# Modulation sums of an MLP stage: halves of the accumulated blocks move past a stationary block of ones, and the rows come back through memory

## The chip, the cores and the metric

One of the eight NeuronCores of a Trainium2 chip runs the whole program in one launch. The metric is the time of one execution on the device in microseconds (us). Engines are named as in the profile: PE is TensorE (matmul), PEld its loads of stationary tiles, DVE VectorE, ACT ScalarE, POOL GpSimd, SP SyncE, which here only issues DMAs. Each engine takes its instructions in the order of its own list and waits on semaphores.

## The reference, cut to what matters

Two transformer blocks of two layers each run on 512 tokens of width 1024; the second also carries 256 context tokens. The first block ends each of its layers with an MLP, and the second block modulates its activations by twelve vectors a layer that come from two condition vectors:

```python
# first block, each layer, 512 tokens: w1 1024x4096, w2 4096x1024
a = relu(h @ w1); x = x + (a * a) @ w2
# second block, each of two layers; c: latent condition, c_ctx: context condition
mod = silu(c) @ ada_w[layer] + ada_b[layer]      # 1024 -> 6144, for both conditions
sh1, sc1, g1, sh2, sc2, g2 = split(mod, 6)
hx = rmsnorm(x, norm1_g) * (1 + sc1) + sh1       # and so on
```

The matrix ada_w is 1024x6144 a layer, 24 MB. The modulation of layer l of the second block depends on no activation, so it can be computed at any time before that layer.

## The kernel before, in words

Activations lie as 128 features on the partitions, 8 groups, 512 tokens in a row. A product in float32 precision is made of three matmuls of type fp32r: each operand is kept as a rounded high half and a low half (the difference), and high x high, high x low, low x high are summed (TERMS). Weights come in blocks of 1 MB, 128 partitions x 2048, numbered in the order of their use (block s is used in step s of what follows). SP loads a block into STG (two buffers), ScalarE rounds it into the high half of HL (two buffers) in two operations of 1024 columns, VectorE subtracts for the low half, in two operations. The function convert(upto) does this in the ScalarE and VectorE programs; start(u) calls convert(u.i + 1). ScalarE may round block s+2 only when PE has finished with block s, since the buffer is the same, and SP loads block s+2 into STG when VectorE has split block s.

The change sits in feed_forward, in the MLPs of the first block (layers l = 0 and 1), which are called with `l` and the buffers FF1. It has one part for each engine: in tensor, scalar and vector. A step is one use of a block: 48 matmuls of 512 columns. Up steps (w1, two for each j of 8) make two tiles of 128 hidden features, down steps (w2, two for each j) make four tiles of the output. The order is up, up, up, up, down, down, up, up, down, down and so on, 32 steps, numbered from 0: steps 2 and 3 are up, 4 and 5 down, 6 and 7 up, 8 and 9 down. Tiles go in pairs into two sets of psum banks in turn; an up step has one pair, a down step two. So the first pair of the second of two down steps needs the banks of the first pair of the down step ahead of it, and waits until VectorE has added that pair to the residual (label "ev").

In an up step VectorE multiplies the two psum tiles through ReLU with the norm's factor (TMP), calls convert(u.i + 2), then modulate(), then subtracts for the low halves of the hidden tiles; ScalarE in between squares and rounds them. In a down step VectorE adds the four tiles, calls convert, then modulate(). Step 0 is special: the norm of the layer's input is not yet known when its matmuls run, so its sum of squares comes behind it on PE (last_sums), ScalarE takes the root's first guess from it (roots: Ln, then Exp), VectorE refines it (newton), and only then can step 0's tiles be evacuated. VectorE's modulate() of step 0 stands ahead of newton.

The modulation is computed beside the MLP, 24 blocks b of 256 columns of ada_w a layer. They are spread over the 32 steps by

```python
mod_steps = [s for s in range(32) if s % 4 != 1 or s < 5 or s > 21][:24]
```

which is steps 0 to 4, then all up to 28 except 5, 9, 13, 17, 21. POOL loads block b (1 MB) into ADA[b % 2] when block b-2 has been used. In step s VectorE multiplies and accumulates it over the 8 groups of inputs, for both conditions c, into ACC[b % 2] (128 x 2 x 256): for group 0 a product (label macc0), then fourteen scalar_tensor_tensor operations. What is left is a sum over the 128 partitions. PE makes it behind the matmuls of step s+1 (its modulate): four matmuls with a 128x128 piece of ACC as the stationary operand and one column of ones moving past it, in plain float32, so that four columns come out in bank 7. VectorE's modulate in step s+1 adds the bias and writes two columns of MOD[l]. The layers of the second block wait for label ("mod", l, 23). MOD[0] is first read after the first block's end, MOD[1] one layer later.

Every operation is recorded by a small wrapper class, so its line in the profile is that of the wrapper: L94 matmul, L97 transpose, L100 activation, L107 tensor_tensor, L111 and L112 tensor_scalar, L115 scalar_tensor_tensor, L118 tensor_copy, L134 dma_start.

## Time and profile before

| | us |
|---|---|
| median of 3 runs | 3605.08 (3603.23 to 3611.28) |
| the profiled execution, its own time | 3599.35 |
| its span, first to last instruction | 3597.6 |
| PE busy | 3436.0 (96%) |
| VectorE busy | 2014.9 (56%) |
| ScalarE busy | 1207.1 (34%) |
| matmuls of one moving column (392 records) | 46.4 busy |

The page comes from one execution; the span leaves out what lies ahead of the first and behind the last instruction, 1.75 us here. A matmul in float32 has two records for each instruction of the program: 48 blocks of 4 are 384 records of one column, and eight more belong to another stage. Matmul records overlap, since their ends are modelled: the time from one start to the next is what a matmul costs, not its record. The operands' fp32r shows in the profile as f32 where it is read.

### The profile page before, as it was taken

How to read it: one execution, taken by the hardware profiler on the slowest of the kernel's cores; microseconds unless marked ns; L12 is line 12 of the kernel's file. 1: busy time of each engine (PE TensorE's matmuls, PEld its weight loads, DVE VectorE, ACT ScalarE, POOL GpSimd, SP SyncE). 2: the span in 40 equal slices, each digit the busy share in tenths (PEclk: the TensorE clock that was granted, in tenths of full speed). 3: DMA queues.
4: the chain of work that ended last, by engine and by line, in shares of the span. 5: the costliest groups of instructions: out<-in, count | busy, mean ns of one | idle time of the engine just before them, and what ended most of it. 6: DMA issues, size and time to landing. Idle time of an engine off the chain costs nothing.

```text
span 3597.6 us, 42138 instructions
## 1 busy us (share of the span) xinstructions
PE 3436.0 (96%) x17456; PEld 2738.1 (76%) x17456; DVE 2014.9 (56%) x3705; ACT 1207.1 (34%) x2017; POOL 227.2 (6%) x314
## 2 busy tenths in 40 slices
PE   7989999999989999999999889999999998899998
PEld 6647688887867688887887567888887885468886
DVE  5564578886664587786125775333335236663334
ACT  5353432224363432224112234332233212243332
POOL 0200100001050010000000001000001000000000
PEclk9999999999999999999999989999999998899999
DMA  5302155442212155453211021121112320123231
GB/s 171 98 24 82 57 166 164 152 152 78 85 31 71 47 165 171 153 167 113 89 59 40 9 81 47 59 66 63 59 61 99 102 71 19 41 60 105 94 94 59
DMA packets 210011, 317.00 MB, mean 88 GB/s; under 512 B 5304, under 2 KB 154426, under 8 KB 208540
## 3 DMA queue, kind: packets, MB, share of 16 engines
q1 hardware_dynamic: 194012, 243.00, 21.0%
q0 software_dynamic: 15808, 71.31, 5.9%
q8 instruction: 137, 2.24, 0.3%
q14 instruction: 54, 0.44, 0.0%
HBM read 300.66 MB, written 14.49 MB: 88 GB/s over the span
## 4 chain that ended last, share of the span: by engine, by line
PE 88%; DVE 8%; ACT 3%; issue 1%; DMA 0%; SPq 0%; DVEq 0%; ACTq 0%
PE ps L94 87%; DVE t L115 3%; ACT t L100 3%; DVE t L107 2%; PE ps L97 1%; DVE t L111 1%; DVE t L125 0%; DVE t L121 0%; DVE t L118 0%; DVE ps L115 0%; DMA t<-in_w_in 0%; DVE ps L107 0%; DMA t<-in_mem 0%; DVE t L112 0%; ACT L100 0%
## 5 line engine op out<-in xcount | busy, mean ns | idle before, releaser
L94 PE MATMUL ps<-t,t 128*128 128x512 f32 (+6 forms) x17040 | 3382.5, 363 | 132.4 <-DVE t L115 45.6
L94 PEld LDWEIGHTS ps<-t,t 128*128 128x128 f32 (+3 forms) x17040 | 2688.3, 188 | 800.1 <-issue 163.8
L100 ACT ACTIVATE t<-t 128x1024 fp32r<-128x1024 f32 (+5 forms) x1158 | 822.1, 744 | 1258.4 <-PE ps L94 935.4
L107 DVE TENSOR_TENSOR t<-t,t 128x1024 fp32r<-128x1024 f32 (+6 forms) x790 | 724.5, 947 | 561.2 <-ACT t L100 555.6
L100 ACT ACTIVATE t<-ps 128x512 f32<-128x512 f32 (+7 forms) x442 | 222.3, 529 | 770.7 <-PE ps L94 736.1
L115 DVE SCALAR_TENSOR_TENSOR t<-t,t,t 128x256 f32<-128x256 f32 (+2 forms) x927 | 438.6, 535 | 18.3 <-ACT t L100 11.6
L107 DVE TENSOR_TENSOR t<-ps,t 128x512 f32<-128x512 f32 (+4 forms) x293 | 188.9, 661 | 205.8 <-PE ps L94 143.6
L115 DVE SCALAR_TENSOR_TENSOR t<-ps,t,t 128x512 f32<-128x512 f32 (+2 forms) x252 | 154.9, 661 | 247.3 <-PE ps L94 227.1
L107 POOL TENSOR_TENSOR t<-t,t 128x64 f32<-128x64 f32 (+2 forms) x208 | 143.6, 713 | 1710.7 <-ACT t L100 1573.3
L118 DVE COPY t<-ps 128x256 f32<-128x256 f32 (+3 forms) x162 | 73.0, 479 | 269.0 <-PE ps L94 253.3
L115 DVE SCALAR_TENSOR_TENSOR t<-ps,t 128x512 f32<-128x512 f32 (+1 forms) x144 | 92.5, 649 | 119.5 <-PE ps L94 106.0
L100 ACT ACTIVATE t<-t,t 128x512 fp32r<-128x512 f32 (+3 forms) x160 | 95.4, 604 | 188.0 <-DVE t L107 127.8
L97 PE MATMUL ps<-t,t 128*128 128x128 f32 x416 | 74.4, 302 | 24.9 <-DMA t<-in_mem 8.2
L111 DVE TENSOR_SCALAR t<-t,t 128x256 f32<-128x256 f32 (+3 forms) x257 | 93.9, 381 | 5.8
L97 PEld LDWEIGHTS ps<-t,t 128*128 128x128 f32 x416 | 52.1, 151 | 54.9 <-issue 12.9
L100 ACT ACTIVATE t<-ps,t 128x256 f32<-128x256 f32 (+3 forms) x88 | 47.5, 544 | 131.0 <-PE ps L94 99.6
L134 POOL DMA_DIRECT2D t<-in_ada_w x48 | 42.7, 890 | 638.6 <-DVE t L115 591.9
L121 DVE TENSOR_REDUCE t<-ps 128x1 f32<-128x512 f32 (+1 forms) x64 | 35.4, 553 | 16.0 <-PE ps L94 15.8
L115 DVE SCALAR_TENSOR_TENSOR t<-t,t,ps 128x128 f32<-128x128 f32 (+1 forms) x96 | 36.1, 380 | 5.3 <-PE ps L94 2.7
L115 DVE SCALAR_TENSOR_TENSOR ps<-t,ps 128x512 f32<-128x512 f32 (+2 forms) x44 | 28.0, 636 | 19.7 <-ACT t L100 17.6
L134 POOL DMA_DIRECT2D t<-gates_away x10 | 6.0, 598 | 512.5 <-PE ps L94 512.5
L112 DVE TENSOR_SCALAR t<-ps 128x256 f32<-128x256 f32 (+1 forms) x42 | 18.2, 433 | 30.5 <-PE ps L94 30.5
(33 smaller groups left out, 296.6 us busy)
## 6 DMA issues: line engine op xcount, KB each, us to landing
t<-in_w_ff SPq DMA_DIRECT2D x64, 1024.0 KB, 5.3
t<-in_w_mlp SPq DMA_DIRECT2D x64, 1024.0 KB, 5.4
t<-in_ada_w POOLq DMA_DIRECT2D x48, 1024.0 KB, 5.8
t<-in_w_in SPq DMA_DIRECT2D x30, 1024.0 KB, 5.3
t<-in_w_qkv_o SPq DMA_DIRECT2D x12, 1024.0 KB, 5.1
t<-in_w_mem_kv SPq DMA_DIRECT2D x8, 1024.0 KB, 6.8
t<-in_w_mem_q SPq DMA_DIRECT2D x8, 1024.0 KB, 5.0
t<-in_w_mem_o SPq DMA_DIRECT2D x8, 1024.0 KB, 5.1
```

What stands on the lines that cost most here:

```text
L94: return Issued(self, self.e and self.e.matmul(o, l, r, start=start, stop=stop, skip_group_check=True))
L97: return Issued(self, self.e and self.e.transpose(o, i, ident))
L100: return Issued(self, self.e and self.e.activation(o, i, f, **kw))
L107: return Issued(self, self.e and self.e.tensor_tensor(o, a, b, op))
L111: return Issued(self, self.e and self.e.tensor_scalar(o, a, s1, None, op0))
L112: return Issued(self, self.e and self.e.tensor_scalar(o, a, s1, s2, op0, op1))
L115: return Issued(self, self.e and self.e.scalar_tensor_tensor(out=o, in0=a, scalar=s1, in1=b, op0=op0, op1=op1))
L118: return Issued(self, self.e and self.e.tensor_copy(o, a))
L121: return Issued(self, self.e and self.e.tensor_reduce(o, a, AX, ALU.max))
L134: return Transfer(self, self.e and self.e.dma_start(dst, src))
```

## The change

PE's four one-column matmuls of a block are replaced by two whose stationary operand is a 128x128 block of ones (ONES, rounded to fp32r by ScalarE at the stage's start) and whose moving operand is ACC itself, 512 columns: first its high half, then its low half (ACH), summed in bank 7. All 128 rows of the bank then hold the same 512 sums. One row of it is the result.

- ScalarE's first_products makes the two products of group 0 (macc0) in step s, which were VectorE's; sums_high rounds ACC into ACH's high half in step s+1, behind convert; sums_row copies one partition of bank 7 to ROW in step s+3. In the up steps these three stand in the order sums_row, first_products, convert, sums_high. In step 0 they stand behind roots.
- VectorE's sums_low subtracts for the low half of ACH in step s+1, behind the ReLUs or adds and ahead of convert. It waits for sums_high (label mhi).
- PE makes the two matmuls behind step s+2, not s+1.
- SP writes the row of block b to mod_rows in device memory behind the issue of weight block s+6 (row_out). When all 24 rows of a layer are there it reads them back as a 24x512 tile into SQ[1] (row_in); PE turns it in four transposes (mod_turn), and VectorE adds the bias in four operations and writes MOD (mod_columns). For layer 0 that is in step 5 of layer 1's MLP (VectorE: step 6), for layer 1 between two uses in the second block's first layer. The label waited for is ("mod", l, 3).

The diff, cut to its core:

```diff
+            f.ACH = [ar([128, 2, 512], R) for _ in range(2)]
+            f.ROW = [ar([1, 512]) for _ in range(2)]
...
+    def mod_turn(pe, l, bk):
+        pe.wait_ge("mod_in", l)
+        for y in range(4):
+            ins = pe.transpose(P[bk][:, 24 * y:24 * y + 24], SQ[1][0:24, 128 * y:128 * y + 128], cst("ident")[0:24, 0:24])
+        ins.then_inc("modT", l)
...
+                if l == 1 and s == 5:
+                    opening(6)
+                    mod_turn(pe, 0, 6)
+                    free[6] = [("mod", 0, 3)]
+                if l is None or s - 2 not in mod_steps:
                     return
-                b = mod_steps.index(s - 1)
-                pe.wait_ge("macc", l, b, 1)
+                b = mod_steps.index(s - 2)
                 opening(7)
-                for m in range(2):
-                    for c in range(2):
-                        ins = pe.matmul(P[7][:, 2 * m + c:2 * m + c + 1], tiles.ACC[b % 2][:, c, 128 * m:128 * m + 128],
-                                        cst("ones", 128, 1), True, True)
-                ins.then_inc("mps", l, b)
-                free[7] = [("mod", l, b)]
+                pe.wait_ge("ones_r", l)
+                pe.wait_ge("mhi", l, b)
+                pe.matmul(P[7][:, :], tiles.ONES[:, :], tiles.ACH[b % 2][:, 0, :], True, False)
+                pe.wait_ge("mlo", l, b)
+                pe.matmul(P[7][:, :], tiles.ONES[:, :], tiles.ACH[b % 2][:, 1, :], False, True).then_inc("mps", l, b)
+                free[7] = [("mrow", l, b)]
...
+            if l is not None:
+                act.activation(tiles.ONES[:, :], cst("ones"), ACT.Copy).then_inc("ones_r", l)
+            def sums_row():
+                s = step[0]
+                if l is not None and s - 3 in mod_steps:
+                    b = mod_steps.index(s - 3)
+                    act.wait_ge("mps", l, b)
+                    if b >= 2:
+                        act.wait_ge("row_away", l, b - 2)
+                    act.activation(tiles.ROW[b % 2][:, :], P[7][0:1, :], ACT.Copy).then_inc("mrow", l, b)
+            def first_products():
+                s = step[0]
+                if l is not None and s in mod_steps:
+                    b = mod_steps.index(s)
+                    act.wait_ge("ada", l, b)
+                    if b >= 2:
+                        act.wait_ge("mlo", l, b - 2)
+                    for c in range(2):
+                        act.activation(tiles.ACC[b % 2][:, c, :], tiles.ADA[b % 2][:, 0:256], ACT.Copy, scale=SIL[:, 0, c:c + 1]).then_inc(
+                            "macc0", l, b, c)
+            def sums_high():
+                s = step[0]
+                step[0] += 1
+                if l is not None and s - 1 in mod_steps:
+                    b = mod_steps.index(s - 1)
+                    act.wait_ge("macc", l, b, 1)
+                    if b >= 2:
+                        act.wait_ge("mps", l, b - 2)
+                    act.activation(tiles.ACH[b % 2][:, 0, :], tiles.ACC[b % 2][:, :, :].rearrange("p c n -> p (c n)"),
+                                   ACT.Copy).then_inc("mhi", l, b)
...
             def up_late(j):
                     start(u)
                     if u is f1[0][0]:
                         roots([((nkey, 0), P[6][:, :], 128, 0, ("sumsq", (nkey, 0), 7))], 1.0 / D)
+                    sums_row()
+                    first_products()
                     convert(u.i + 2)
+                    sums_high()
                     for x, t in enumerate(u.tiles):
                         act.wait_ge("ev", u.n, t.m, 0)
...
                     up(j + 1)
                 for b, u in enumerate(f2[j]):
                     start(u)
+                    sums_row()
+                    first_products()
+                    if l is not None and j < 7:
+                        convert(u.i + 2)
+                    sums_high()
                     if j == 7:
...
+    def mod_columns(dve, l, bk):
+        dve.wait_ge("modT", l)
+        for y in range(4):
+            c, m = y // 2, y % 2
+            dve.tensor_tensor(MOD[l][:, m::2, c], P[bk][:, 24 * y:24 * y + 24], vec(f"ada_b{l}", 0, 48)[:, m::2], ALU.add).then_inc(
+                "mod", l, y)
...
+            def sums_low():
+                if l is not None and step[0] - 1 in mod_steps:
+                    b = mod_steps.index(step[0] - 1)
+                    dve.wait_ge("mhi", l, b)
+                    dve.tensor_tensor(tiles.ACH[b % 2][:, 1, :], tiles.ACC[b % 2][:, :, :].rearrange("p c n -> p (c n)"),
+                                      tiles.ACH[b % 2][:, 0, :].bitcast(F), ALU.subtract).then_inc("mlo", l, b)
...
-                if l is not None and s - 1 in mod_steps:
-                    b = mod_steps.index(s - 1)
-                    dve.wait_ge("mps", l, b)
-                    for m in range(2):
-                        k = 2 * b + m
-                        ins = dve.tensor_scalar(MOD[l][:, k, :], P[7][:, 2 * m:2 * m + 2], vec(f"ada_b{l}", k), None, ALU.add)
-                        if m == 0:
-                            ins.then_inc()
-                        else:
-                            ins.then_inc("mod", l, b)
+                if l == 1 and s == 6:
+                    mod_columns(dve, 0, 6)
...
-                            if kk == 0:
-                                dve.tensor_scalar(o, w, x, None, ALU.mult).then_inc("macc0", l, s, c)
-                            else:
+                            if kk > 0:
                                 dve.wait_ge(*(("macc0", l, s, c) if kk == 1 else ("maccp", l, s, kk - 1, c)))
                                 ins = dve.scalar_tensor_tensor(o, w, x, o, ALU.mult, ALU.add)
...
+                        if not first:
+                            sums_low()
                         convert(u.i + 2)
                         if not first:
                             modulate()
...
                             early_newton("n1_1", 0, S)
+                    sums_low()
                     if l is not None and j < 7:
                         convert(u.i + 2)
...
+        rows_at = {U.ff[l][0][0][0].i + s + 6: (l, b) for l in range(2) for b, s in enumerate(mod_steps)}
+        rows_back = {U.ff[1][0][0][0].i + 4: (0, ("ff1", 0)), U.gg[0][1].i: (1, ("n1_0", 0))}
+        def row_out(l, b):
+            sp.wait_ge("mrow", l, b)
+            sp.dma_start(A["mod_rows"][l, b:b + 1, :], FF1.ROW[b % 2][:, :]).then_inc(s_row[b % 2], "row_away", l, b)
+        def row_in(l, key):
+            sp.wait_ge("row_away", l, 22)
+            sp.wait_ge("row_away", l, 23)
+            sp.wait_ge("sumsq", key, 7)
+            sp.dma_start(SQ[1][0:24, :], A["mod_rows"][l]).then_inc(s_mod, "mod_in", l)
...
+                if done[0] in rows_back:
+                    row_in(*rows_back[done[0]])
                 done[0] += 1
...
+                if done[0] in rows_at:
+                    row_out(*rows_at[done[0]])
```

## Rows read from the trace of the kernel before

**Rows 1.** The page: busy time and share of each engine; the chain by engine.
```profile
PE 3436.0 (96%) x17456; PEld 2738.1 (76%) x17456; DVE 2014.9 (56%) x3705; ACT 1207.1 (34%) x2017; POOL 227.2 (6%) x314
...
PE 88%; DVE 8%; ACT 3%; issue 1%; DMA 0%; SPq 0%; DVEq 0%; ACTq 0%
```

**Rows 2.** Busy time of each engine in two stretches, the MLPs of layers 0, 1.
```profile
core 0: us, PE busy (x) PEld busy (x) DVE busy (x) ACT busy (x) POOL busy (x), PEclk, DMA share, GB/s
466.00:822.00 356.00, 356.00 (x1627) 290.35 (x1627) 295.25 (x602) 102.13 (x132) 19.08 (x22) 1.00 0.46 151
1290.00:1646.00 356.00, 356.00 (x1628) 290.33 (x1627) 295.27 (x602) 99.39 (x128) 19.87 (x22) 1.00 0.47 154
```

**Rows 3.** ScalarE in order of time, 523 to 575 us: start, us, what, idle before.
```profile
537.49 4.39 ACT L100 ACTIVATE t<-t 128x1024 fp32r<-128x1024 f32 x6 [10.09 <-PE ps L94]
548.69 4.39 ACT L100 ACTIVATE t<-t 128x1024 fp32r<-128x1024 f32 x6 [6.81 <-PE ps L94]
560.78 2.01 ACT L100 ACTIVATE t<-t 128x1024 fp32r<-128x1024 f32 x2 [7.70 <-PE ps L94]
572.88 2.01 ACT L100 ACTIVATE t<-t 128x1024 fp32r<-128x1024 f32 x2 [10.08 <-PE ps L94]
```

**Rows 4.** PE by shape, whole span; then the same from 548.4 to 549.3.
```profile
L97 PE MATMUL ps<-t,t 128*128 128x128 f32 x416 | 74.4, 302 | 24.9 <-DMA t<-in_mem 8.2 <-DVE t L111 6.8 <-DVE t L115 5.8
...
L94 PE MATMUL ps<-t,t 128*128 128x1 f32 x392 | 46.4, 239 | 0.0
...
L94 PE MATMUL ps<-t,t 128*128 128x1 f32 x8 | 0.9, 239 | 0.0
```

**Rows 5.** VectorE in order of time, 535 to 563 us.
```profile
538.59 2.36 DVE L107 TENSOR_TENSOR t<-t,t 128x1024 fp32r<-128x1024 f32 x2 [0.46 <-ACT t L100]
...
548.15 1.28 DVE L115 SCALAR_TENSOR_TENSOR t<-ps,t 128x512 f32<-128x512 f32 x2
549.78 2.36 DVE L107 TENSOR_TENSOR t<-t,t 128x1024 fp32r<-128x1024 f32 x2 [0.35 <-ACT t L100]
552.06 0.34 DVE L111 TENSOR_SCALAR t<-ps,t 128x2 f32<-128x2 f32 x2
552.32 0.61 DVE L111 TENSOR_SCALAR t<-t,t 128x256 f32<-128x256 f32 x2
552.84 5.63 DVE L115 SCALAR_TENSOR_TENSOR t<-t,t,t 128x256 f32<-128x256 f32 x14
558.39 1.28 DVE L107 TENSOR_TENSOR t<-t,t 128x512 fp32r<-128x512 f32 x2
559.60 2.47 DVE L107 TENSOR_TENSOR t<-ps,t 128x512 f32<-128x512 f32 x4
```

**Rows 6.** ScalarE by shape, whole span; then DMA issues by tensor with us to landing.
```profile
L100 ACT ACTIVATE t<-ps 128x512 f32<-128x512 f32 (+7 forms) x442 | 222.3, 529 | 770.7 <-PE ps L94 736.1
...
L100 ACT ACTIVATE t<-t,t 128x256 f32<-128x256 f32 x64 | 32.4, 508 | 22.3 <-DVE t L125 22.2
...
L100 ACT ACTIVATE t<-t 128x512 f32<-128x512 f32 x35 | 21.6, 618 | 1.3 <-DVE t L115 1.3
...
t<-in_w_ff SPq DMA_DIRECT2D x64, 1024.0 KB, 5.3
...
t<-in_ada_w POOLq DMA_DIRECT2D x48, 1024.0 KB, 5.8
...
out<-t SPq DMA_DIRECT2D x4, 512.0 KB, 2.6
```

**Rows 7.** All engines in order of time, 457 to 480 us: step 0's end, layer 0.
```profile
458.19 5.63 DVE L115 SCALAR_TENSOR_TENSOR t<-t,t,t 128x256 f32<-128x256 f32 x14
...
465.77 0.69 ACT L100 ACTIVATE t<-ps,t 128x512 f32<-128x512 f32 x1 [9.47 <-PE ps L94]
466.50 2.53 ACT L100 ACTIVATE t<-t 128x512 f32<-128x512 f32 x3
466.50 0.70 DVE L112 TENSOR_SCALAR ps<-ps 128x512 f32<-128x512 f32 x1 [2.68 <-ACT t L100]
...
470.77 3.55 DVE L107 TENSOR_TENSOR t<-t,t 128x1024 fp32r<-128x1024 f32 x4
...
477.03 3.20 ACT L100 ACTIVATE t<-t 128x1024 fp32r<-128x1024 f32 x4 [4.24 <-PE ps L94]
```

**Rows 8.** PE behind two waits, and granted clock (before the DMA share) in stretches behind.
```profile
378.89 0.33 PE L97 MATMUL ps<-t,t 128*128 128x128 f32 x1 [2.76 <-DVE t L111]
...
1969.04 6.38 PE L94 MATMUL ps<-t,t 128*128 128x512 f32 x32 [2.39 <-DVE t L107]
...
380.00:384.00 4.00, 4.00 (x12) 0.57 0.02 4
...
1969.00:1976.00 7.00, 6.96 (x34) 1.00 0.02 5
```

More of the change, by code:

```diff
@@ L188, in program @@
     s_bias = [sem("bias_landed0"), sem("bias_landed1")]
+    s_row, s_mod = [sem("mod_row_away0"), sem("mod_row_away1")], sem("mod_landed")
     s_mask = sem("mask_landed")
@@ L468, in ff_area @@
             f.ACC = [ar([128, 2, 256]) for _ in range(2)]
+            f.ACH = [ar([128, 2, 512], R) for _ in range(2)]
+            f.ROW = [ar([1, 512]) for _ in range(2)]
         return f
     FF1, FF2 = ff_area(S, True), ff_area(S + C, False)
+    FF1.ONES = place([128, 128], R, D1 + 57344)
     SQC = [place([128, C], F, D1 + b) for b in (57344, 60544)]
@@ L761, in modulate @@
                 step[0] += 1
-                if l is None or s - 1 not in mod_steps:
+                if l == 1 and s == 5:
[3 more added lines that the diff above has]
+                if l is None or s - 2 not in mod_steps:
                     return
-                b = mod_steps.index(s - 1)
-                pe.wait_ge("macc", l, b, 1)
+                b = mod_steps.index(s - 2)
                 opening(7)
-                for m in range(2):
-                    for c in range(2):
-                        ins = pe.matmul(P[7][:, 2 * m + c:2 * m + c + 1], tiles.ACC[b % 2][:, c, 128 * m:128 * m + 128],
-                                        cst("ones", 128, 1), True, True)
-                ins.then_inc("mps", l, b)
-                free[7] = [("mod", l, b)]
+                pe.wait_ge("ones_r", l)
[4 more added lines that the diff above has]
+                free[7] = [("mrow", l, b)]
             def up(j):
@@ L1068, in hybrid_tensor @@
         feature(U.gd[l], HR2, x)
+        if l == 0:
+            opening(7)
+            mod_turn(pe, 1, 7)
+            free[7] = [("mod", 1, 3)]
         feature(U.gk[l], HR2, x)
@@ L1446, in feed_forward @@
             f1, f2 = ff
-            at_t = [0]
+            at_t, step = [0], [0]
+            if l is not None:
[28 more added lines that the diff above has]
+                                   ACT.Copy).then_inc("mhi", l, b)
             def up_late(j):
@@ L2405, in modulation @@
         def modulation(which, name):
-            dve.wait_ge("mod", l, 23)
+            dve.wait_ge("mod", l, 3)
             o = 24 * which
@@ L2445, in hybrid_vector @@
         start(u)
+        if l == 0:
+            mod_columns(dve, 1, 7)
         for t in u.tiles:
@@ L3046, in build @@
         A[name] = nc.dram_tensor(name, (128, n), F).ap()
+    A["mod_rows"] = nc.dram_tensor("mod_rows", (2, 24, 512), F).ap()
     A["bounce"] = nc.dram_tensor("bounce", (16 * 64 * 465 + 256,), F).ap()
```

## The prediction

> **What bounds the kernel now.** I read the page first. TensorE works 96% of the span and 88% of the chain that ended last; VectorE has 8% of that chain, ScalarE 3% [rows 1]. The change lives in two stretches, the MLPs of the first block, and in the second view both look alike: in 356 us TensorE is busy 356.00 us at full clock, VectorE 295 us, ScalarE 102 us [rows 2]. So every TensorE microsecond taken out there comes off the end, and every microsecond that TensorE waits is put on it. VectorE has 17% left on average, but an average says nothing of an order of waits.
>
> I call one use of a weight block a step: 32 steps a layer, 48 products of 512 columns each. ScalarE starts to round block s+2 when TensorE has ended step s, so its starts are a clock: 537.49, 548.69, 560.78, 572.88 [rows 3]. A step without sums matmuls takes 11.20 us (0.2333 us a product), one with them 12.09, so the eight narrow records behind it [rows 4] cost 0.89 us. I name A the start of ScalarE's rounding at the end of a step. TensorE's first product of the next step starts at A - 0.25: ScalarE starts 0.09 behind the last product's end, and products that last 0.40 follow each other at 0.2333.
>
> The rows of VectorE through one second up step (s=7, A=548.69) are the heart [rows 5]. Its two ReLUs are over at 549.4; low halves of block s+2 549.78 (they wait for ScalarE's high halves); two 128x2 evictions 552.06; two first products 552.32; fourteen multiply-adds 552.84; two hidden low halves 558.39; and only at 559.60 = A + 10.91 the first add of step 8's results. Step 9 writes the bank which that add empties. The add ends at A + 11.6, TensorE wants the bank at A - 0.25 + 0.89 + 11.20 + 0.89 = A + 12.73. TensorE never waits in these rows, but by 1.1 us only.
>
> **The change part by part.**
> *Matmuls.* 48 times 0.89 us go; 48 times two moves of 512 columns come, 2 x 0.2333 = 0.47. The loads of stationary tiles lie beside products as they do now, 290 us of loads under 356 [rows 2]. 48 x 0.42 = 20.3 us less, all on the path. Bounds: if the pair rides for nothing, 42.7; if each costs 0.40, the length of a record that overlaps with nothing, 4.3. I take the spacing (also 1627 products in 356 us, 0.22) [rows 2], as these are the same products as their neighbours. The Trainium skill (TensorE: Matmul & The Clock Gate, Back-to-back issue gap) gives N/2.4 + 2.5 ns, 216 ns at 512; that would be an estimated 1.6 us less still. The trace's 233 ns is used.
>
> *Turns.* Two times four small transposes. The 416 transposes of before keep TensorE 74.4 us, 0.18 each; the narrowest records 0.12 [rows 4]: eight are 1.4 us (0.9 to 2.4). The waits before them are for DMAs sent at least two steps earlier; a landing takes 2.6 us for small stores and 5.3 for a block [rows 6]. Their eight VectorE adds (0.2 us each, by the 128x2 evictions, two in 0.34) [rows 5] fall into a step that starts with slack. Rows written from SP: each waits for ScalarE's row of block b and stands behind weight block s+6, in front of s+7. That row is ready some 6 us after step s+2 ends, and s+7 can be loaded only when VectorE has split s+5, about 17 us after. Nothing: the weight stream has 12 us of cover there, and were the cover gone each row would cost the wait left over.
>
> *ScalarE.* A block adds two scaled copies of 128x256 (0.51 in another stage, about 0.4 spaced), one rounding of 128x512 (0.62) and one eviction (0.53, the 128x512 eviction) [rows 6]: about 1.9 us in a step of 11.7 in which ScalarE does 102 x 11.2/356 = 3.2. Room enough. The scaled copies wait for the ada block, which lands about 6 us behind the macc of two blocks earlier [rows 6], half a step before it is wanted.
>
> *VectorE's order.* Per block two evictions (0.26) and two first products (0.52) go; one 128x512 subtraction (0.60) comes. By busy time VectorE gains 0.2. But the subtraction stands ahead of convert and waits for mhi, which ScalarE makes only behind both high halves of the weights. Walk it for s=7: ScalarE's two roundings are spaced 0.96, so mhi starts at A + 1.91 and is there at A + 2.55; VectorE (free at A + 0.7) subtracts from A + 2.6 to 3.2, splits the weights to 5.48 (2.28), does fourteen multiply-adds to 11.03 (5.55), hidden lows to 12.24 (1.21), and the first add ends at 12.93; with a semaphore and the restart of TensorE about 0.15, step 9 starts at A + 13.1. TensorE could start at A - 0.25 + 11.20 + 0.47 = A + 11.42 (step 5 was skipped by mod_steps, so step 7 has no pair behind it). It waits 1.65 us. This holds where a second up step with a block is followed by two down steps, and the step two before it has no block: step 9, 13, 17, 21 and 25. Before steps 5 and 29 there is a pair more of TensorE work, so 1.2. A layer: 5 x 1.65 + 2 x 1.2 = 10.65; two layers 21.3 us. Bounds: 0 (ScalarE or VectorE shorter by the whole 1.65) and 14 x 2.5 = 35, if mhi also comes behind work of the step before. I take the walk, which is made of rows of the very place. In steps of other kinds the same delay is hidden: VectorE is 0.6 us late at the next ReLU and waits for mhi anyway.
>
> *First step.* Now VectorE accumulates block 0 while it waits for the norm's sums, 458.19 to 463.8, and Newton's first operation is at 466.50 [rows 7]. In the changed order ScalarE makes the first products only behind Ln (465.77) and Exp (466.50), and VectorE's accumulation, which stands ahead of Newton, waits for them: macc0 at 467.5, fourteen operations to 473.1, then what took 466.50 to 470.77 (less 0.1 of waiting) to 477.3, two weight splits to 479.6. TensorE needs that block for step 2 and has ended step 1, whose pair is gone, so that it wants it at 477.03 - 0.25 = 476.8. It waits 3.0 us, once a layer: 6.0. Step 2's own sums come later and by then VectorE has caught up. Bounds 2.5 and 4.0 (if the two scaled copies take as long as 512 columns). A wait of about this length was followed by the lower clock, 1.2 GHz: 2.76 us idle to 378.89, then a mean of 0.57 over 4 us (3.4 of them at half speed), while 2.39 us at 1969.04 was followed by a clock of 1.00 [rows 8]. 3.4 us at half speed lose 1.7; in two layers 3.4. Bounds 0 and 7.
>
> Sum: -20.3 + 1.4 + 21.3 + 6.0 + 3.4 = +11.8. The profiled execution took 3599.35 us (span 3597.6); it should go to 3611.1. The median shown, 3605.08, is 5.7 above that execution, and I give the result on its scale: 3616.9, so 3617.
>
> **Rivals.**
> *A, the matmuls alone count.* VectorE finishes a block no later, because ScalarE's rounding slips in earlier or the operations are tighter than I space them; only the first step stalls: -20.3 + 1.4 + 6.0 + 3.4 = -9.5, 3595.6. For it: 61 us of VectorE are free [rows 2] and its busy time falls. Against it: the free time lies before the ReLUs, not in the 10.9 us behind A [rows 5], and each hop of the walk is a queue in order. The Trainium skill (VectorE: DVE Perf Modes, Rules for kernel authors) says to minimize the count of operations, not semaphores. By that rule this change, 18 operations to 15 a block, helps VectorE. The trace agrees for semaphores of VectorE on itself (fourteen chained multiply-adds at 0.396 each) [rows 5], and shows 0.35 to 0.46 us of idle where it waits for ScalarE.
>
> *B, half of it.* The restart is cheaper and the wait shorter by 0.8 a place: stalls 10.6 instead of 21.3, 3606.2, no difference to be seen.
>
> *C, everything hidden*, the first step too, if Newton were not behind the accumulation: -18.9, 3586.2. The order of the code speaks against it.
>
> *D, worse.* The delay feeds on itself in the seven blocks without a gap (steps 22 to 28): ada blocks are asked for later, ScalarE waits for them ahead of its weights. From 5 us of lateness on, TensorE waits for weights in each of these steps; 2 us in 2 x 4 steps is 16 more, 3633. Against it: VectorE's step sums to 11.1 us of work, TensorE's to 11.67, so lateness shrinks.
>
> **How the numbers follow.** Forecast 0.60 (its own range 3609 to 3623), A 0.15, B 0.15, C 0.05, D 0.05. What a measurement can tell from no change is about 0.2%, 7.2 us: slower from 3612.3 on, faster below 3597.9. Slower: 0.90 of the forecast's 0.60, D, and a little of B: 0.60. Same: the rest of the forecast and nearly all of B: 0.21. Faster: A (most) and C: 0.19. The range from 3602 to 3624 leaves A, C and D out.
>
> **What would show it.** Right: the narrow records gone; steps 11.20 and 11.67 by ScalarE's clock, except step 8 and its like, where the clock is stretched; TensorE idle 1.0 to 1.7 us ahead of steps 5, 9, 13, 17, 21, 25, 29 with a VectorE add as its releaser; and about 3 us once a layer, ahead of step 2, released by a weight split, with a dip of the clock behind it. The down step's add after a second up step starts 12.2 us behind A instead of 10.9. Wrong: TensorE still 356.00 busy in the stretch; the subtraction starting before A + 2; a stall on mlo, mrow or the turns, on which my sum puts nothing.

## The result

The changed kernel takes 3622.62 us (median of 6 runs, 3620.59 to 3633.28) against 3607.26 (6 runs) for the kernel before: 1.0041 times as long, with a 95% interval of 1.0027 to 1.0055. By this ratio it is 14.8 us more (9.7 to 19.8). The forecast was 11.8 us more, slower, and 3617 in a range of 3602 to 3624.

The page of the profile after (its own time 3623.28) answers to [rows 1]: TensorE a little more busy, but a smaller part of the chain that ended last, and VectorE 12% of it instead of 8%.

```profile
span 3621.5 us, 41796 instructions
...
PE 3442.2 (95%) x17176; PEld 2728.5 (75%) x17176; DVE 2003.6 (55%) x3569; ACT 1293.4 (36%) x2211; POOL 226.0 (6%) x314
...
PE 83%; DVE 12%; ACT 4%; issue 1%; DMA 0%; POOL 0%; SPq 0%; ACTq 0%; DVEq 0%; POOLq 0%
```

The two MLP stretches, where TensorE had not a gap in 356 us [rows 2], now have 12 us of idle each. ScalarE went from 102 to 141 us. The waits of TensorE in the first stretch are eight, all for VectorE's L107 (one line each of the stretches; engine waited for: us in total, times, longest):

```profile
466.00:822.00 356.00, 343.92 (x1463) 274.58 (x1461) 294.82 (x545) 141.25 (x221) 19.43 (x22) 1.00 0.46 151
1290.00:1646.00 356.00, 343.93 (x1465) 273.48 (x1464) 288.07 (x534) 141.96 (x223) 19.44 (x22) 1.00 0.47 157
```
```profile
PE ps L94 <- DVE t L107: 12.1, 8, 2.8
```

VectorE's order around the end of step 7, which answers to [rows 5], and TensorE at the same place. ScalarE starts its rounding (my A) at 552.05.

```profile
552.05 4.91 ACT L100 ACTIVATE t<-t 128x1024 fp32r<-128x1024 f32 x7 [6.00 <-PE ps L94]
```
```profile
551.29 1.40 DVE L115 SCALAR_TENSOR_TENSOR t<-ps,t 128x512 f32<-128x512 f32 x2 [0.70 <-PE ps L94]
554.61 2.96 DVE L107 TENSOR_TENSOR t<-t,t 128x512 fp32r<-128x512 f32 x3 [1.93 <-ACT t L100]
557.49 5.62 DVE L115 SCALAR_TENSOR_TENSOR t<-t,t,t 128x256 f32<-128x256 f32 x14
563.03 1.29 DVE L107 TENSOR_TENSOR t<-t,t 128x512 fp32r<-128x512 f32 x2
564.24 2.48 DVE L107 TENSOR_TENSOR t<-ps,t 128x512 f32<-128x512 f32 x4
```
```profile
559.72 3.89 PE L94 MATMUL ps<-t,t 128*128 128x512 f32 x16
565.07 5.14 PE L94 MATMUL ps<-t,t 128*128 128x512 f32 x21 [1.45 <-DVE t L107]
```

The second row of VectorE is the new subtraction and the two weight splits merged: it begins after 1.93 us of waiting for ScalarE, at A + 2.56, where the splits began at A + 1.09 after 0.35. The add that frees the bank begins at A + 12.19 instead of A + 10.91, and TensorE goes on at A + 13.02. A row of the view joins many products, and their records overlap. So I read a gap from starts: from the start of the last product before this gap to the start of the first behind it the trace has 1.85 us, where neighbours have 0.23.

Step 0 of layer 0, against [rows 7]: fourteen multiply-adds stand behind Exp and in front of Newton's first operation, and TensorE is idle for 2.83 us ahead of step 2.

```profile
466.35 0.63 ACT L100 ACTIVATE t<-t 128x512 f32<-128x512 f32 x1
466.88 0.89 ACT L100 ACTIVATE t<-t,t 128x256 f32<-128x256 f32 x2
467.48 5.63 DVE L115 SCALAR_TENSOR_TENSOR t<-t,t,t 128x256 f32<-128x256 f32 x14 [9.68 <-ACT t L100]
...
473.03 0.68 DVE L112 TENSOR_SCALAR ps<-ps 128x512 f32<-128x512 f32 x1
...
477.21 3.55 DVE L107 TENSOR_TENSOR t<-t,t 128x1024 fp32r<-128x1024 f32 x4
...
479.62 2.93 PE L94 MATMUL ps<-t,t 128*128 128x512 f32 x6 [2.83 <-DVE t L107]
```

**Where the time went.** I cut the executions at the moments at which SP issues fixed weight blocks (in the first profile of before 447.5, 885.1, 936.5, 1271.2, 1802.3, 1872.2, 2219.6 and 3538.3 us) and compare the lengths of the pieces with that profile, in us. I call the piece from 936 to 1271 us, in layer 1 of the first block, the attention, and the one from 1872 to 2220, the second block's first mixer, the mixer:

```
piece of the first profile of before: layer 0's MLP  attention  layer 1's MLP     mixer         later
                                        448 to 885   936 to 1271  1271 to 1802   1872 to 2220  2220 to 3538
changed kernel                            +4.9         +8.3          +5.1           +8.2          -2.5
changed kernel, second profile            +7.1         +3.1          +4.8          +11.4          -2.6
kernel before, second profile              0.0         -0.1          +0.4          +16.5          +0.3
```

The third row is the same program as the first profile. Its mixer alone was 16.5 us longer, and what differs is TensorE's granted clock (before the DMA share: 0.93, then 0.88):

```profile
1872.00:2220.00 348.00, 311.62 (x1750) 0.93 0.13 43
```
```profile
1872.00:2220.00 348.00, 316.16 (x1704) 0.88 0.13 43
```

So the mixer's 8.2 us need no effect of the change, and 24 us between the two profiled executions are not the result: the first profile of before was a lucky execution, 8 us below its median. What the change certainly did is in the two MLPs, 10.0 us (11.9 in the second profile). There is something more in the attention, which is taken up below, and the last piece is 2.2 to 2.6 us shorter in seven of the eight profiles of kernels with the wide matmuls and in none of the five others, which I did not follow up.

Two profiles are few, but the record has the span and the mean granted clock of 231 executions. The granted clock has two levels here, 2.4 and 1.2 GHz, so an execution's time at the lower one is its span times twice what the mean lacks of 1. Within one kernel, an execution is 0.38 us longer for each us more of it. An estimate follows from these numbers. The mean of the kernel before is 3611.8 us with 191 us at the lower clock (108 executions), that of the changed kernel 3624.3 with 210 (6 executions): 12.4 us apart, of which 7 go with the clock. On the chip of experiment 11 the two are 15.6 apart, with 221 against 195 us at the lower clock, of which 10 go with it. At equal clock the changed kernel thus loses 5 to 6 us. The rest of the 14.8, about 9, is more time at the lower clock.

### The profile page after: what moved, and what is told of

Same layout as the page of the kernel before. It is cut to its first block, busy times and chain, and to the rows that moved or that the text cites. A ratio compares the mean times of both kernels' runs of the same rounds, so it can differ in the third digit from the quotient of the medians.

```text
span 3621.5 us, 41796 instructions
## 1 busy us (share of the span) xinstructions
PE 3442.2 (95%) x17176; PEld 2728.5 (75%) x17176; DVE 2003.6 (55%) x3569; ACT 1293.4 (36%) x2211; POOL 226.0 (6%) x314
## 4 chain that ended last, share of the span: by engine, by line
PE 83%; DVE 12%; ACT 4%; issue 1%; DMA 0%; POOL 0%; SPq 0%; ACTq 0%; DVEq 0%; POOLq 0%
PE ps L94 82%; DVE t L115 6%; DVE t L107 4%; ACT t L100 4%; PE ps L97 1%; DVE t L111 1%; DVE t L121 0%; DVE ps L115 0%; DVE t L118 0%; DVE t L125 0%; DVE ps L107 0%; DMA t<-gates_away 0%; DMA t<-in_mem 0%; DVE t L112 0%; ACT L100 0%
## 5 line engine op out<-in xcount | busy, mean ns | idle before, releaser
L100 ACT ACTIVATE t<-t 128x1024 fp32r<-128x1024 f32 (+6 forms) x1208 | 846.4, 737 | 1174.0 <-PE ps L94 836.1
L107 DVE TENSOR_TENSOR t<-t,t 128x1024 fp32r<-128x1024 f32 (+5 forms) x838 | 752.5, 930 | 602.6 <-ACT t L100 596.7
L100 ACT ACTIVATE t<-ps 128x512 f32<-128x512 f32 (+6 forms) x490 | 249.6, 533 | 779.2 <-PE ps L94 744.8
L107 DVE TENSOR_TENSOR t<-ps,t 128x512 f32<-128x512 f32 (+5 forms) x301 | 186.7, 646 | 203.2 <-PE ps L94 137.2
L107 POOL TENSOR_TENSOR t<-t,t 128x64 f32<-128x64 f32 (+2 forms) x208 | 142.8, 710 | 1716.0 <-ACT t L100 1570.8
L100 ACT ACTIVATE t<-t,t 128x256 f32<-128x256 f32 (+3 forms) x256 | 138.3, 562 | 201.3 <-DVE t L107 125.9
L97 PE MATMUL ps<-t,t 128*128 128x128 f32 (+1 forms) x424 | 76.8, 305 | 24.4 <-DMA t<-in_mem 7.9
L97 PEld LDWEIGHTS ps<-t,t 128*128 128x128 f32 (+1 forms) x424 | 53.5, 153 | 56.2 <-issue 15.0
L111 DVE TENSOR_SCALAR t<-t,t 128x256 f32<-128x256 f32 (+3 forms) x161 | 64.8, 403 | 5.8
L121 DVE TENSOR_REDUCE t<-ps 128x1 f32<-128x512 f32 (+1 forms) x64 | 35.3, 552 | 15.7 <-PE ps L94 15.5
```

The lines of the kernel that those rows point to most:

```text
L97: return Issued(self, self.e and self.e.transpose(o, i, ident))
L100: return Issued(self, self.e and self.e.activation(o, i, f, **kw))
L107: return Issued(self, self.e and self.e.tensor_tensor(o, a, b, op))
L111: return Issued(self, self.e and self.e.tensor_scalar(o, a, s1, None, op0))
L121: return Issued(self, self.e and self.e.tensor_reduce(o, a, AX, ALU.max))
```

## The experiments

Each run is compared with executions of the kernel before on the same chip. T, R1, R2, K and L are the theories that the expectations name. A gap is the time from the start of one product to the start of the next where TensorE stood still; 0.23 is none.

**1. First products ahead of the root, in step 0 only.**

```diff
                     if u is f1[0][0]:
+                        first_products()
                         roots(...)
                     sums_row()
-                    first_products()
+                    if u is not f1[0][0]:
+                        first_products()
```

> The changed kernel, but in step 0 ScalarE makes block 0's two first products ahead of the norm's Ln and Exp. Theory T (the loss sits in waits of VectorE's queue, 3.0 us in front of step 2 of each layer and 1.2 to 1.65 us in front of seven down steps): the 3.2 us gap between two products ahead of step 2 goes, and with it the dip of the clock where there was one; the seven others stay. 3622.6 - 6.0 - 1.7 = 3615. Rival R1 (VectorE's total work of the first steps, not the place of the first products, holds step 2 up): the gap stays, or comes back before step 3 or 5; 3621 to 3623.

3616.96 us, ratio 1.0012 (0.9997 to 1.0027). The gap of 3.23 us ahead of step 2 is gone in both layers, the seven others stand to the hundredth (1.39, five of 1.85, 1.39), and the waits in the stretch fell from eight to seven:

```profile
PE ps L94 <- DVE t L107: 9.2, 7, 1.5
```

The MLPs took +0.5 and +2.1 us against before, instead of +4.9 and +5.1: 7.4 us less, forecast 7.7. The median is 2 us above the 3615 expected. R1 is out: what held step 2 was the place of two small products in ScalarE's list.

**2. The subtraction behind convert.**

```diff
-                        if not first:
-                            sums_low()
                         convert(u.i + 2)
+                        if not first:
+                            sums_low()
```

(and the same swap in the down steps)

> The changed kernel, but VectorE subtracts for ACH's low half behind convert instead of ahead of it, so that it no longer waits for ScalarE's rounding with the weights behind it. Theory T: the first add behind a second up step starts near A + 10.7 instead of A + 12.2; the gaps of 1.6 us ahead of steps 9, 13, 17, 21, 25 shrink to 0.2 or less, those of 1.2 ahead of 5 and 29 go; 21.3 us less one or two: 3622.6 - 20 = 3602 to 3603. Rival R1 (the added ScalarE and VectorE work itself costs the time, wherever it stands): under 5 us less, 3618 or more. Rival R2 (rows through memory and later stages cost it): no change, 3621 to 3624.

3617.29 us, ratio 1.0007 (0.9989 to 1.0024). I had expected 3602 to 3603, so in the total the theory missed by 15 us. At the place of the edit it held. VectorE waits 0.46 us for ScalarE, not 1.93, and its first add begins at 561.77, with the splits at 552.14 = A + 1.09, so at A + 10.72:

```profile
552.14 2.96 DVE L107 TENSOR_TENSOR t<-t,t 128x1024 fp32r<-128x1024 f32 x3 [0.46 <-ACT t L100]
555.03 5.63 DVE L115 SCALAR_TENSOR_TENSOR t<-t,t,t 128x256 f32<-128x256 f32 x14
560.57 1.29 DVE L107 TENSOR_TENSOR t<-t,t 128x512 fp32r<-128x512 f32 x2
561.77 0.69 DVE L107 TENSOR_TENSOR t<-ps,t 128x512 f32<-128x512 f32 x1
```
```profile
PE ps L94 <- DVE t L107: 2.8, 1, 2.8
```

Of eight waits one is left, step 2's. The MLPs are 5.2 and 3.4 us shorter than before, 18.6 shorter than in the changed kernel (forecast 20). The profiled execution does not show it in its total, because its attention took 15.9 us more and its mixer 16.5 more, both at a lower clock. It was the slowest of twelve; the three fastest took 3601.34 to 3602.28, as expected. By the estimate above this kernel is 13 us below before at equal clock, but it had the most time at the lower one, 228 us.

**3. Both edits**, a version meant to beat both kernels.

> Both edits: first products of block 0 ahead of the norm's root, and the subtraction behind convert. Theory T: the MLP stages hold only the gain of the matmuls, -20.3 + 1.4 for the turns + 1.5 of rest, 17 us below the kernel before, 3590; TensorE waits nowhere in the two MLPs for over 0.3 us. Rival R1: 3610 or more. Rival R2 (the later stages really became slower by some 5 to 10 us, which the sum of the MLP stages does not explain): 3595 to 3600.

3597.79 us, ratio 0.9964 (0.9949 to 0.9979): 13 us below the kernel before, by the two ratios 28 below the changed one. Theory T wanted 3590, and the median lies in the band of R2, which had later stages 5 to 10 us slower. TensorE has no wait left in the stretches:

```profile
466.00:822.00 356.00, 356.00 (x1524) 285.26 (x1523) 296.72 (x540) 150.25 (x234) 22.42 (x24) 1.00 0.46 151
1290.00:1646.00 356.00, 356.00 (x1529) 285.18 (x1529) 295.24 (x541) 144.37 (x226) 25.00 (x26) 1.00 0.46 151
```

The MLPs are 9.6 and 8.5 us shorter than before, 18.1 together (forecast 17). So the wide matmuls themselves gain, and two places in two queues had made a loss of them. But R2 is right in part: in the profile the attention took 4.4 of the 18 us back, and over twelve executions this kernel spent 205 us at the lower clock against 191, some 5 us; at equal clock it is an estimated 19 us below before.

**4. Group 0's products back on VectorE.**

```diff
-                            if kk > 0:
+                            if kk == 0:
+                                dve.tensor_scalar(o, w, x, None, ALU.mult).then_inc("macc0", l, s, c)
+                            else:
```

> The changed kernel, but with group 0's two products back on VectorE in every block. Theory T: no wait of 3 us ahead of step 2 (minus 6.0 and minus 1.7 of clock), but VectorE's chain is 0.52 us longer at 14 places (gaps of 2.1 and 1.7 instead of 1.6 and 1.2), plus 7.3: 3622.2, nothing to be seen in the time and all of it in the gaps. Rival R1 (VectorE has free time, 17% of the stretch, so 0.52 us a block costs nothing): 3615.

3628.99 us, ratio 1.0052 (1.0036 to 1.0068), where I had expected 3622.2. The gap ahead of step 2 is gone, the seven others are 2.38 and 1.91 instead of 1.85 and 1.39: 0.52 us each, as much as two products take of VectorE [rows 5], though VectorE is free for 60 us of this stretch.

```profile
708.52 3.81 PE L94 MATMUL ps<-t,t 128*128 128x512 f32 x10 [1.98 <-DVE t L107]
```
```profile
710.00:713.00 3.00, 3.00 (x9) 0.52 0.57 206
```

The row of the second view has the granted clock behind this wait, 0.52 as a mean of 3 us (1.2 GHz for most of them): three of the ten waits of 1.98 us in the two stretches were followed by such a piece of 3.4 us, and none of the four of 1.52. I had not put that in; this makes the MLPs +5.8 and +8.4 instead of even with the changed kernel.

**5. One wide matmul instead of two.**

```diff
-                pe.matmul(P[7][:, :], tiles.ONES[:, :], tiles.ACH[b % 2][:, 0, :], True, False)
                 pe.wait_ge("mlo", l, b)
-                pe.matmul(P[7][:, :], tiles.ONES[:, :], tiles.ACH[b % 2][:, 1, :], False, True).then_inc("mps", l, b)
+                pe.matmul(P[7][:, :], tiles.ONES[:, :], tiles.ACH[b % 2][:, 0, :], True, True).then_inc("mps", l, b)
```

> The changed kernel with one wide matmul a block instead of two (the low half is still made and waited for, but left out of the sum, so the modulation is only as exact as fp32r). Theory T: 0.233 us less at each of 48 places for TensorE, but the waits ahead of steps 9, 13, 17, 21, 25 grow by 0.233 each and those ahead of 5 and 29 by 0.467, because VectorE's chain sets the end there: 9 of 24 pairs a layer give nothing. 2 x 15 x 0.233 = 7.0 less, gaps between products of 2.08 and 1.86 instead of 1.85 and 1.39. The two MLPs together 7.0 us shorter than in the changed kernel. Rival R1 (TensorE's own time sets these stages everywhere): 11.2 us less, gaps unchanged.

3622.08 us, ratio 1.0026 (1.0009 to 1.0042). The gaps are 2.08 and 1.85, within a hundredth as said: TensorE's time was taken out, and where VectorE's chain sets the end it came back as waiting.

```profile
PE ps L94 <- DVE t L107: 14.2, 8, 2.8
```

The MLPs took +3.0 and +3.2: 3.8 us less than in the changed kernel, not 7.0. The clock accounts for the difference: behind the waits ahead of step 2 it was low for 6.8 and 3.4 us, in the changed kernel for 3.4 and 0, which is 3.4 us of time.

**6. The halves alone, added to the kernel before.** ScalarE's sums_high and VectorE's sums_low as in the change, results unused, the four narrow matmuls kept. As in the change, ScalarE's convert of a down step moves up with sums_high.

```diff
+                    sums_high()      # ScalarE, behind convert
...
+                        if not first:
+                            sums_low()   # VectorE, ahead of convert
                         convert(u.i + 2)
```

> The kernel before, with only the two halves of ACC added as in the change: ScalarE's rounding behind convert, VectorE's subtraction ahead of convert, both results unused; matmuls, first products and evictions as before. Theory T: VectorE's first add behind a second up step moves from A + 10.9 to A + 13.0, ends at 13.7, and TensorE, ready at A + 12.7, waits 1.1 us at each of 7 places a layer: gaps of 1.35 between products that now follow without one, 15.7 us in all over the two MLPs. Rival R1 (the change's loss comes from its wide matmuls, rows or first products): no gap over 0.5 ahead of a down step, the MLPs as long as before.

3629.63 us, ratio 1.0044 (1.0029 to 1.006). The kernel before, which never waited here, now waits at the seven places, for the same releaser:

```profile
554.55 2.96 DVE L107 TENSOR_TENSOR t<-t,t 128x512 fp32r<-128x512 f32 x3 [1.83 <-ACT t L100]
...
564.97 2.47 DVE L107 TENSOR_TENSOR t<-ps,t 128x512 f32<-128x512 f32 x4
```
```profile
565.70 2.60 PE L94 MATMUL ps<-t,t 128*128 128x512 f32 x10 [0.75 <-DVE t L107]
```

ScalarE's rounding starts at 552.00 here, so the add begins at A + 12.97, and 13.0 was forecast. Its gaps are 1.00, not 1.35; a part of the delay now falls ahead of the narrow matmuls (gaps of 0.3) and of the product behind the restart (0.34). The sum is right: the MLPs took +7.8 and +8.3, forecast 15.7. R1 is out: the two halves alone, without wide matmuls, rows or ScalarE's first products, bring the waits. The same edit that costs the changed kernel 1.6 us a place costs this one 1.1: the narrow matmuls give TensorE 1.3 us more to do in that window, and VectorE's own products and evictions take 0.8 of it.

**7. The kernel before once more**, unchanged.

> The kernel before, unchanged, profiled once more. The four runs so far gave MLP stages as theory T has them, but kernels whose MLPs end at other times all spent 8 to 17 us more than the first profile of before between 1866 and 2240 us (same instructions, more time at the lower TensorE clock). Theory K (that stage's clock depends on when it comes): this execution comes at the same times as the first, so it shows the same lower-clock pieces near 1947, 1991, 2035, 2049, 2080, 2093, 2121, within a few us of the same length, and a span near 3598 to 3603. Rival L (the first profile was simply a lucky one): this one shows the longer pieces of the changed kernels (17 us, 14 us near 2010 and 2060), span 3605 to 3612.

3610.79 us, ratio 0.9992 (0.9976 to 1.0008). The table above has its pieces. For the mixer theory K fails and L holds: 16.5 us between two executions of one program that reach it at the same time to 0.2 us. For the attention the two agree to 0.1 us.

**8 and 9. Idle matmuls in layer 0's MLP of the kernel before**, four, then two.

```diff
                 free[7] = [("mod", l, b)]
+                if l == 0 and s == 12:
+                    opening(6)
+                    for _ in range(4):
+                        pe.matmul(P[6][:, :], cst("ones"), CST[:, 0:512], True, True)
```

> The kernel before with four idle float32 matmuls of 512 columns (0.43 us each, 1.7 us) behind one step of layer 0's MLP, their result unused. Theory K (stages behind lose or win TensorE clock by the time at which they come): the total changes by clearly more or less than 1.7 us, and the neighbourhood attention or the stage from 1866 to 2240 takes 5 us or more longer than in the first profile of before. Rival L (clock pieces are drawn anew in each execution, no matter when the stage comes): +1.7 on the median of before, 3609 to 3612, in the mean.

3613.84 us, ratio 1.0007 (0.9991 to 1.0022). The MLP was 3.4 us longer, twice what I had said, since each of these is two records (eight for four below). The attention took -0.1, the mixer +3.4.

```profile
609.86 3.68 PE L94 MATMUL ps<-t 128*128 128x512 f32 x8
```

> The kernel before with two idle float32 matmuls behind one step of layer 0's MLP. Such a matmul has two records of 0.43 us and costs 0.86 us (four of them came to 3.4 us, not 1.7), so this is 1.7 us. So far the stage from 936 to 1271 us (layer 1's neighbourhood attention and memory attention) took the same time to 0.1 us in three profiles, of kernels that reach it 0, 0 and 3.4 us late, and 4.4 to 15.9 us more in seven that reach it at other times (-9.6, -5.2, +0.5, +3.0, +4.9, +5.8, +7.8). Theory K (the clock given in that stage hangs on when it comes): 1.7 us late is another such time, and the stage takes 4 us or more longer. Rival L (kernels with the added work lose it for another reason, for which the plain kernel before has no cause): the stage takes as long as before to 0.5 us.

3623.67 us, ratio 1.0018 (0.9998 to 1.0039). The attention took 3.2 us more, with two pieces of lower clock in it (near 1024 and 1089 us) that the two profiles of before and that of experiment 8 do not have. This is neither "4 or more" nor "as before to 0.5". So in one execution at least the attention was longer without any of the change's work. The median is 13.6 us above that of before on this chip, for 1.7 us of idle work; the ratio says 6.5, and the twelve executions lie between 3603.71 and 3633.94.

**10. Both edits, and twelve idle wide matmuls** (2.8 us) in layer 0's MLP.

```diff
                 pe.wait_ge("mlo", l, b)
+                if l == 0 and s == 12:
+                    opening(6)
+                    for _ in range(12):
+                        pe.matmul(P[6][:, :], tiles.ONES[:, :], tiles.ACH[b % 2][:, 0, :], True, True)
```

> The kernel with both edits (first products early, subtraction behind convert) and twelve idle wide matmuls, 2.8 us, in layer 0's MLP, so that the attention comes 6.8 us earlier than in the kernel before and not 9.6. Theory K: the stage from 936 to 1271 falls back to its length in the kernel before (4.4 us less than with both edits alone), which more than pays for the 2.8 us. Rival L: that stage stays 4 us or more above before, and the total rises by 2.8.

3597.95 us, ratio 0.9963 (0.9946 to 0.9979), the same as both edits alone, with 2.8 us of idle work in it. The attention took 2.9 us more than before, where K wanted 0 and L over 4: so it speaks for neither.

**11. The changed kernel once more.**

> The changed kernel once more, unchanged. Theory K: the stage from 936 to 1271 us is again 8 us longer than in the kernel before, with a piece of lower clock near 995 us; the stage from 1872 to 2220, which gave 0 and +16.5 us in two profiles of the very same kernel, may come out anywhere between. Rival L (all pieces of lower clock are drawn anew): the first stage comes out at any value from 0 to 16. Both: MLP stages +4.9 and +5.1 us, median 3619 to 3626.

3629.59 us, ratio 1.0040 (1.0024 to 1.0057) against before on its chip, the same loss as in the result. The median itself is above the 3619 to 3626 expected here. The waits are the same eight, 12.1 us. Layer 0's MLP took 7.1 us more and not 4.9, with 6.8 us at the lower clock behind the wait ahead of step 2, where the first profile had 3.4. The attention took +3.1 this time, not 8.3, so K's "again 8" is wrong too.

**The attention over all thirteen profiles.** Against the first profile of before it took 0, -0.1 and -0.1 us in the two profiles of before and in experiment 8, and 2.9 to 15.9 more in the ten others; 3.1 and 8.3 are one and the same kernel. When it starts does not sort them: experiment 8 reaches it 4.5 us after the first profile of before and took nothing more, experiment 1 reaches it 0.5 after and took 6.0 more, the changed kernel 4.8 after and took 8.3 more. The time at the lower clock inside it goes with it: 3.4 us in the three, 10.2 in experiments 9 and 10 (3.2 and 2.9 more), 27.3 in the changed kernel and 47.8 in experiment 2 (15.9 more). The stretch in the first profile of before, in the changed kernel and in experiment 2, with the granted clock before the DMA share:

```profile
936.00:1271.00 335.00, 313.54 (x1715) 0.99 0.18 57
```
```profile
936.00:1271.00 335.00, 315.87 (x1680) 0.96 0.17 53
```
```profile
936.00:1271.00 335.00, 316.87 (x1644) 0.93 0.16 50
```

## Why the prediction was right

*Matmuls, 20.3 us less.* One support of this term was misread: 1627 records in 356 us give 0.22 only because 192 of them are narrow ones. The spacing of 0.2333 does not rest on it. In the kernel with both edits nothing but this gain, the turns and a rest of 0.16 us at five places is left; the forecast for that kernel's MLPs was 17 less, they took 18.1 less.

*Waits ahead of seven down steps, 21.3 us more.* Walked: 1.65 and 1.2. Measured: gaps of 1.85 and 1.39, less the usual 0.23, so 1.62 and 1.16, at exactly the seven steps named, in both layers. 2 x (5 x 1.62 + 2 x 1.16) = 20.8. The walk is the part that the runs bear out best. Its times were subtraction at A + 2.6 (2.56), add at 12.24 (12.19), restart at 13.1 (13.02).

*Step 0, 6.0 us more, and the clock 3.4.* The gap is 3.23 in both layers: 3.0 each. The clock fell behind it in layer 0, not in layer 1 (granted clock is the number before the DMA share):

```profile
479.60:483.60 4.00, 3.98 (x11) 0.62 0.73 222
```
```profile
1316.00:1320.00 4.00, 3.48 (x15) 1.00 0.54 171
```

In four profiles with this wait the clock fell in six of eight cases, for 3.4 or 6.8 us. The term is 1.7 here, not 3.4.

*Turns, 1.4 us more.* Eight small transposes, 0.8 us busy, so the term is nearer 1; no engine waited for the rows' way through memory:

```profile
L97 PE MATMUL ps<-t,t 24*128 24x24 f32 x8 | 0.8, 220 | 0.0
```

*Sum for the MLPs*: -20.3 + 20.8 + 6.0 + 1.7 + about 1 = +9.2; the pieces say 10.0. So the mechanism is the one forecast, and without the clock the MLPs took 8.3 us more, where 8.4 were forecast.

*Where it was luck.* The forecast total, 11.8, and the measured one, 14.8 with an interval of 5 to either side, are made of different parts. The forecast had 8.4 of work and waits and 3.4 of clock, all in the MLPs. By the estimate from all executions 5 to 6 are there at equal clock, 2.5 us less than the MLPs alone, as the last piece is shorter by that much, and about 9 are more time at the lower clock. Of these, 1.7 (3.4 in the second profile) lie behind the waits ahead of step 2. The rest lies elsewhere, part of it in the attention (8.3 and 3.1 us in the two profiles), and no step of the prediction spoke of it. The median, 3622.62, is 1.4 us inside the range, and that of the changed kernel in experiment 11, 3629.59, is outside.

Why the lower clock comes more often is open. It is not the waits in the MLPs alone, since the kernel with both edits has none of them and still 205 us at the lower clock against 191. Whether it needs the change's work at all is not settled: the kernel with two idle matmuls had 205 against 195 (experiment 9), a difference near the scatter of its twelve executions, and the one with four had none more (experiment 8).

*Rivals.* A is what experiment 2 is, with the wait ahead of step 2 alone left: its MLPs took -8.6 us, A said -9.5 for the sum. C is what experiment 3 is, -18.1 against -18.9. So what decided against them was the order of the queues, as was said. B wanted half of the 21.3 us of waits, and 20.8 were there. D's feedback did not come: the waits of step 29, behind seven blocks in a row, are as short as those of step 5. The Trainium skill's rule to minimize the count of operations (VectorE: DVE Perf Modes, Rules for kernel authors) holds at this place for the two products that left VectorE: back on it, they lengthen each of the seven gaps by 0.52 us (experiment 4). It could not make up for the wait for ScalarE, which grew from 0.35 to 1.93 us.

## What to carry to other kernels

An operation added in front of a queue's urgent work costs its own time plus that of whatever it waits for; look for the place behind the urgent work before moving anything. Free time on average says little: find the hop with the smallest slack (here 1.1 us), walk it with the rows of that very place, and remember that shortening the engine in front makes the slack smaller too. A first step has its own order and needs its own walk.

## What the runs showed that I had not expected

The same program spent 16.5 us more in one 350 us stage in one execution than in another, at a granted clock of 0.88 against 0.93; a comparison of two single profiles can be off by more than this whole change. The lower clock came not only behind waits of 2.8 us, but behind three of ten waits of 1.98 us (experiment 4), each costing an estimated 1.7 us more than the wait, half of 3.4. A float32 matmul of 512 columns costs 0.86 us (experiment 8: eight records 0.43 apart for four of them) where an fp32r one costs 0.23.
